# Recurrence levels of both pairs of heads in one step of the weight walk, and every second step empty

## The reference

```
def hgrn2_branch(q, z_fwd, z_bwd, i, g, lb, gain):
    qh = silu(heads(q)); vh = heads(i)
    k_f, lf_f = gates(z_fwd, lb[0])
    k_b, lf_b = gates(z_bwd, lb[1])
    o = chunk_scan(qh, k_f, vh, lf_f) + rev(chunk_scan(rev(qh), rev(k_b), rev(vh), rev(lf_b)))
    o = o * rsqrt(mean(o * o) + EPS)        # per head
    return o * gain * silu(g)
```

## Time and profile before

| | us |
|---|---|
| runs, median | 818.51 |
| runs, all | 818.51, 819.53, 818.17 |
| the profiled execution: span | 817.8 |
| TensorE busy | 803.5 |
| VectorE busy | 643.0 |
| ScalarE busy | 497.9 |
| GpSimd busy | 123.8 |

### The profile page before, as it was taken

How to read it: one execution, slowest core, us unless ns; L and a number is a source line. 1 busy time by engine, 2 the same in 40 slices (tenths; PEclk the granted TensorE clock), 3 DMA queues, 4 the chain that set the end, 5 groups by cost and what they waited for, 6 DMA issues and landing times.

```text
span 817.8 us, 17229 instructions
## 1 busy us (share of the span) xinstructions
PE 803.5 (98%) x6996; PEld 787.0 (96%) x6996; DVE 643.0 (79%) x1022; ACT 497.9 (61%) x891; POOL 123.8 (15%) x137
## 2 busy tenths in 40 slices
PE   6999999999999999999999999999999999999996
PEld 6999999989999999999999999999999999999996
DVE  7788599977987878786998898887987568566673
ACT  6575566756677465655666744555676457566652
POOL 0022255401040000000240620001203130000001
PEclk9999999999999999999999999999999999999998
DMA  9934544466667989898777567675765336455441
GB/s 337 382 96 140 165 142 122 154 195 205 194 201 235 355 304 342 305 324 331 249 249 252 164 208 219 216 260 179 207 180 167 127 122 189 177 155 156 149 130 53
DMA packets 47022, 170.42 MB, mean 208 GB/s; under 512 B 5216, under 2 KB 5472, under 8 KB 46688
## 3 DMA queue, kind: packets, MB, share of 16 engines
q1 hardware_dynamic: 46224, 165.31, 61.8%
q10 hardware_dynamic: 720, 4.01, 1.2%
HBM read 168.26 MB, written 1.05 MB: 207 GB/s over the span
## 4 chain that ended last, share of the span: by engine, by line
PE 92%; DVE 4%; ACT 1%; DMA 1%; POOL 1%; issue 0%; SPq 0%; POOLq 0%; DVEq 0%; ACTq 0%
PE bank L196 91%; DVE wl L235 2%; DMA raw<-in_ws 1%; POOL sq L235 1%; DVE raw L223 0%; PE bank L199 0%; ACT wh L205 0%; SPq L193 0%; ACT sq L202 0%; DVE B0l L223 0%; DVE h L223 0%; DVE B1l L235 0%; ACT B1h L202 0%; ACT B0h L202 0%; DVE gd L235 0%
## 5 line engine op out<-in xcount | busy, mean ns | idle before, releaser
L235 DVE TENSOR_TENSOR wl<-raw,wh 128x1024 fp32r<-128x1024 f32 (+1 forms) x260 | 327.6, 1273 | 22.6 <-ACT wh L205 21.5
L205 ACT CAST wh<-raw 128x1024 fp32r<-128x1024 f32 (+1 forms) x260 | 269.0, 1046 | 105.2 <-DMA raw<-in_ws 53.7
L196 PE MATMUL bank<-XAh,wl 128*128 128x256 f32 (+1 forms) x896 | 254.7, 284 | 0.1
L196 PE MATMUL bank<-XAl,wh 128*128 128x256 f32 (+1 forms) x896 | 249.0, 278 | 0.0
L196 PE MATMUL bank<-XAh,wh 128*128 128x256 f32 (+1 forms) x896 | 248.8, 278 | 0.0
L196 PEld LDWEIGHTS bank<-XAh,wl 128*128 128x128 f32 x896 | 168.4, 188 | 3.1 <-issue 1.3
L196 PEld LDWEIGHTS bank<-XAh,wh 128*128 128x128 f32 x896 | 168.6, 188 | 0.1
L196 PEld LDWEIGHTS bank<-XAl,wh 128*128 128x128 f32 x896 | 168.6, 188 | 0.0
L196 PE MATMUL bank<-B1h,wl 128*128 128x256 f32 (+1 forms) x464 | 129.3, 279 | 0.0
L196 PE MATMUL bank<-B1l,wh 128*128 128x256 f32 (+1 forms) x464 | 128.7, 277 | 0.0
L196 PE MATMUL bank<-B1h,wh 128*128 128x256 f32 (+1 forms) x464 | 128.6, 277 | 0.0
(11 more groups left out here) (276 smaller groups left out, 1219.6 us busy)
## 6 DMA issues: line engine op xcount, KB each, us to landing
raw<-in_ws SPq DMA_DIRECT2D x306, 512.0 KB, 4.5
bias<-in_bias ACTq DMA_DIRECT2D x1, 1664.0 KB, 12.0
hK<-in_xk SPq DMA_DIRECT2D x4, 272.0 KB, 5.4
h<-in_xt ACTq DMA_DIRECT2D x1, 1088.0 KB, 7.4
out<-gd SPq DMA_DIRECT2D x4, 256.0 KB, 2.6
raw<-in_ws SPq DMA_DIRECT2D x2, 256.0 KB, 3.9
C<-in_cst SPq DMA_DIRECT2D x1, 512.0 KB, 8.5
crow<-in_crow ACTq DMA_DIRECT2D x1, 512.0 KB, 6.0
```

The lines of the kernel that those rows point to most:

```text
L196: return self.real.matmul(*a, **k)
L205: return self.real.copy(*a, **k)
L235: return self.real.tensor_tensor(*a, **k)
```

## The change

`in_turn` takes one generator a step. The new `abreast` advances all of them in one step and then yields as many times as there are generators, so that the count of steps stays the same. It replaces `in_turn` around the levels on TensorE, ScalarE, VectorE and GpSimd, with nothing else changed.

```diff
+def abreast(*runs):
+
+    runs = list(runs)
+    while runs:
+        n = len(runs)
+        for r in list(runs):
+            try:
+                next(r)
+            except StopIteration:
+                runs.remove(r)
+        if runs:
+            for _ in range(n):
+                yield
...
-                yield from in_turn(levels(0), levels(1))
+                yield from abreast(levels(0), levels(1))
...
```

## The result

| | before | after |
|---|---|---|
| median of the runs taken side by side | 818.50 (20 runs) | 820.06 (20 runs) |
| ratio, 95% interval | | 1.0018 (1.0011 to 1.0025) |
| profiled execution: span | 817.8 | 818.2 |
| first burst of the recurrence to the product with iN of head 0 | 63.20 | 63.99 |

By the interval of the ratio that is 0.9 to 2.0 us more. Against the forecast's 819.1 (0.6 more than 818.51) it is 1.0 to the slow side, and inside the range. The last line of the table is the yardstick of all that follows. It is 63.20 in three kernels with the old order (before, runs 6 and 8).

What follows compares the result with a forecast made beforehand. TensorE was taken as the bound (busy 803.5 of 817.8 us). 2.0 us saved on its bursts and 2.6 lost waiting for VectorE's low halves gave +0.6 on 818.51, about 819.1 us, range 816.9 to 821.2.

Steps and rivals of the forecast that it cites:

- Sign and place: Recurrence: no measurable difference, leaning slower by 0.6 us, with double bursts and TensorE waiting for wl before units 10 and 12.
- Term 1: TensorE, units 4 to 18: merging two bursts saves 0.25 us per pair, 2.0 us over 8 pairs (1.7 to 2.5).
- Term 2: VectorE's pieces ahead of even units' subtractions: TensorE waits 1.43 us at unit 10, 1.20 at unit 12, 2.6 in all.
- The interference: VectorE's two-input products run slower beside GpSimd's kf and kb, adding 1.1 us up to unit 10.
- by order alone: Pieces moved ahead of subtractions, without added GpSimd slowing: waits of 0.33 us at unit 10, 1.20 at unit 12, 1.5 together.
- 1.9 us are left: ScalarE's copies for the joined burst's second group: wanted 3.55 us earlier, released 1.15 earlier, still 1.9 us of cover.
- The rival: ScalarE's copies come late and TensorE waits before double bursts: 2.6 us in all, 821.1 us; chance 0.05.
- VectorE as the bound of every pair: Subtractions for units 12 to 20: a pair takes 7.3 to 7.4 us, 3.1 slower in all, 821.6; chance 0.21.
- The sum against the median: The +0.6 us on the 817.8 span was put on the median 818.51, 0.7 above that span: about 819.1.

Runs made afterwards that it cites:

- run 6: Kernel before the change, with GpSimd's products of kf and kb cut to one column of one group: 819.21 us, ratio 0.9998.
- run 8: Kernel before the change, with VectorE's subtraction one unit earlier (AHEAD 4 instead of 3): 854.74 us, ratio 1.0434.
- run 5: Changed kernel, with GpSimd's products of kf and kb cut to one column of one group: 816.24 us, ratio 0.9965.
- run 4: Changed kernel, with VectorE's double piece one step later, behind the subtraction for the even unit: 817.67 us, ratio 0.9994.
- run 2: Changed kernel, with VectorE alone put back to taking turns and the other three engines left abreast: 818.35 us, ratio 0.9995.
- run 7: Changed kernel, with VectorE's subtraction one unit earlier (AHEAD 4 instead of 3): 851.71 us, ratio 1.0398.
- run 10: Kernel before, with TensorE's bursts alone joined and VectorE's merge into AT moved to the end of its piece: 820.97 us, ratio 1.0026.
- run 3: Changed kernel, with TensorE alone put back to taking turns: 821.30 us, ratio 1.0036.
- run 12: Kernel before, with TensorE's bursts alone joined and GpSimd's products of kf and kb cut to one column: 817.09 us, ratio 0.9976.
- run 9: Kernel before, with TensorE's bursts alone joined, in the odd step, the first pair's burst one unit later: 821.09 us, ratio 1.0030.
- run 11: Kernel before, with only VectorE's merge into AT moved to the end of its piece: 820.62 us, ratio 1.0025.

## Why the prediction was right

**Sign and place** held: a change of 0.18%, leaning to slower, with double bursts, and waits for wl before units 10 and 12 (1.92 and 0.66, where 1 to 1.5 was forecast for each). That the sum came out near (0.6 forecast, 0.8 in the stretch) is in part luck: both terms were too small, by 0.9 and by 1.1, and the errors cancel. The 1.6 between the medians lies 1.0 above the forecast, and 0.8 of the 1.6 isn't explained by either term.

- **Term 1** was put at 0.25 for a pair, with 0.31 as the upper bound, and measured 0.36. The step that failed is the split of a burst's 0.81 into entry and filling. I took 16 spacings of 0.031 (0.50) from the records' length, and deducted up to 0.1 for a seam. A joined burst takes 142.97 to 144.48, 1.51 less two spacings of 0.114, or 1.28: the second sixteen cost 0.47, and the seam between two banks nothing that shows. 8 x 0.36 = 2.9 against 2.0, 0.4 over the bound. Runs 5 and 6 confirm it as 2.93.
- **Term 2** was put at 2.6 and measured 3.7. Unit 10: 1.43 forecast, 2.20 lost. It could have started 0.11 after the last matmul of unit 9 (130.38) and starts at 132.57, 2.08 late; 0.11 more goes in the first spacing behind the wait. Counted from the first burst, about a third of the 0.65 between 1.43 and 2.08 is TensorE, which arrives earlier by the larger term 1. The rest is the low half, which comes later: GpSimd costs VectorE 1.6 more than before (5.0 against 3.4), where 1.1 was put. Unit 12: 1.20 forecast, 0.93 lost. Unit 16: nothing forecast, 0.59 lost. The forecast let VectorE keep up there with 6.78 against 6.85 for a pair; against 6.74 it doesn't quite.
- **The interference** was put at 1.1 of 2.6, order at 1.5. Runs 4 and 5 show that this can't be divided: each alone taken away ends all of the waits for wl. The 1.5 "by order alone" was worked out from a VectorE that GpSimd had already slowed by 3.4.
- **"1.9 us are left" for the copies** failed. It compared the copies with the burst at one late level, and didn't count that TensorE's savings add up to 2.9. Where the waits for wl are gone (1, 2, 4, 7), copies or the first sum are late for the second half of two to five bursts and keep 0.8 to 2.0 of the 2.9. In the changed kernel the waits for wl held TensorE back so far that this never showed: the last copy ends 3.7 to 3.9 ahead of the second half of its burst, and 3.7 is what the waits for wl add up to. The rival's chance of 0.05 was too low for the mechanism, though not for this kernel.
- **VectorE as the bound of every pair** didn't come in the changed kernel: behind unit 16 a pair takes 6.74 (157.25 to 163.99) again. One experiment (10) made it, by 0.4 per level.
- **The sum against the median.** The time outside the span is 1.8 to 1.95 in the profiled executions of which both are known (820.15 for a span of 818.2). The 0.7 between span and median was thus no fixed quantity: by that the profiled execution of before took about 819.7 and was one of the longer ones. Adding the difference to the median, as was done, is not touched by that.

Of the versions that compute all of it only run 1, TensorE's bursts joined and all else in turn, is faster than before by more than its interval: 817.05, a ratio of 0.9983. Moving VectorE's pieces ahead of the subtraction as well was what made the waits for wl (runs 2 and 4).

## What to carry to other kernels

Joining small bursts on the bounding engine is a change to that engine's order alone; let the others follow only as far as their results are wanted earlier, and look at what then stands ahead of the work that the bound engine waits for. Where VectorE and GpSimd run side by side, a piece isn't a sum of durations: what stands beside what decides, and an operation that reads a bank is the one to put beside GpSimd's product. When one wait is removed, the next one is found in the trace with the wait gone, not in the one with it (the cover of 1.9).

## What was not expected of the hardware

- **A seam between two float32 bursts** of different banks and operands costs nothing that shows (1.28 for 32 records, 0.81 for 16).
- **A wait costs more than its bracket.** The pair of steps with the wait of 1.92 is 2.20 longer, that with 0.66 0.93, and that with 0.29 0.59: 0.3 more each. More than half of that is in how the bracket counts. It begins at the end of the record before it, and a record of 0.28 is followed by the next start after 0.11: from 130.38 to 132.57 are 2.19; less 0.28 that is the bracket, less 0.11 the 2.08 lost. So lateness of up to 0.17 shows in no bracket. The other 0.11 is real: the second matmul behind the wait comes 0.23 after the first instead of 0.11. In run 3 the waits come behind a burst, where this 0.22 is spent anyway (131.77 to 131.99 in the kernel before), and the next burst moves by only 0.1 more than the bracket.
- **TensorE's matmuls come in two spacings** at a granted clock of 1.00 in both. Three take 0.34 in most units. In run 12 from 115 to 127 us, in run 9 from 113 to 134 and in run 11 from 150 to 174 they take 0.353, which adds 0.4 to 0.6 to the stretch; a pair of steps takes 6.94 instead of 6.74 there. The place near 478 us is the same thing: 0.353 from 478 to 519 in the kernel before, 0.34 in run 1. From the chain, the same 778 matmuls in the kernel before:

```profile
477.86 90.15 PE bank L196 x778
```

and in run 1:

```profile
475.88 89.00 PE bank L196 x778
```

The times of the four kernels with the shorter trace don't show these 1.2 us: against before they differ by their stretch to within 0.4 (run 1: -1.8 and -1.40; run 9: +1.9 and +2.3; run 10: +2.3 and +2.01; run 12: -2.1 and -1.80). That speaks for the execution and against the kernel as the cause, and the 21 runs of the kernel before beside run 10 alone spread from 817.51 to 819.50. But the four are just those in which TensorE alone joins its bursts, there is one trace of each, and none of the other ten traces is short there. What sets the spacing stays open; no run varied it by itself.
